# A two-block transformer layer on one core: scan in two stages, choice of tokens in halves, and two hand-overs moved

## The reference, cut to what matters

```python
# mlstm_scan, for a chunk, from the carried state c0, n0, m0
logw = where(tril, cum[:, None] - cum[None, :] + ic[None, :], -inf)
s = (qc @ kc.T) * exp(logw - m)
num = s @ vc + dec * (qc @ c0);  den = s.sum(-1) + dec * (qc @ n0)
hc = num / maximum(abs(den), exp(-m))
c_new = dn * c0 + (wa * kc).T @ vc;  n_new = dn * n0 + (wa * kc).sum(0)
# branch_merge
x = x + ga1 * ((gates[:D] * y_f + gates[D:] * y_m) @ w_out)
# expert_choice, cap = 128 tokens of 1024 for each of 16 experts
aff = softmax(h @ w_router);  vals, idx = top_k(aff.T, cap)
# second block
x = x + mixed @ w_out;  z = rms_norm(x, ln_g) @ w_in      # the next layer
```

## Time and profile before

| | us |
|---|---|
| median of 3 runs (lowest, highest) | 3307.52 (3302.03, 3307.57) |
| profiled execution (its span) | 3307.75 (3305.9) |
| PE busy | 2930.8 (89%) |
| DVE busy | 1666.1 (50%) |
| ACT busy | 1278.3 (39%) |
| POOL busy | 114.2 (3%) |

### The profile page before, as it was taken

How to read it: one execution, slowest core, us unless ns; L and a number is a source line. 1 busy time by engine, 2 the same in 40 slices (tenths; PEclk the granted TensorE clock), 3 DMA queues, 4 the chain that set the end, 5 groups by cost and what they waited for, 6 DMA issues and landing times.

```text
span 3305.9 us, 37686 instructions
## 1 busy us (share of the span) xinstructions
PE 2930.8 (89%) x13860; PEld 2081.0 (63%) x13860; DVE 1666.1 (50%) x3240; ACT 1278.3 (39%) x2362; POOL 114.2 (3%) x154
## 2 busy tenths in 40 slices
PE   7999977899989179999996798799999978999999
PEld 3454456578868156776663575477667865776677
DVE  2127535334335866666662556743652446645523
ACT  2101222223314154554552545643652446535522
POOL 0000000000000001110010000000000000000000
PEclk9999978999989589999998899899999988999999
DMA  9420000022232469999997110020012020200121
GB/s 356 132 77 0 26 26 1 0 102 102 79 139 109 152 222 356 361 363 368 365 363 201 67 26 26 20 59 23 30 52 102 13 77 14 77 1 33 52 77 51
DMA packets 176664, 388.56 MB, mean 118 GB/s; under 512 B 7028, under 2 KB 8084, under 8 KB 176256
## 3 DMA queue, kind: packets, MB, share of 16 engines
q1 hardware_dynamic: 157920, 318.79, 27.6%
q0 software_dynamic: 18448, 67.72, 6.2%
q10 hardware_dynamic: 144, 0.01, 0.0%
HBM read 354.98 MB, written 31.51 MB: 117 GB/s over the span
## 4 chain that ended last, share of the span: by engine, by line
PE 80%; DVE 8%; ACT 5%; DMA 4%; issue 2%; SPq 1%; POOL 0%; DVEq 0%; POOLq 0%; ACTq 0%
PE psum L292 19%; PE psum L699 7%; PE psum L701 7%; PE psum L700 7%; PE psum L1215 4%; PE psum L1331 4%; PE psum L1217 4%; PE psum L1216 4%; PE psum L1349 3%; PE psum L1160 3%; PE psum L1159 3%; PE psum L1158 3%; PE psum L1378 2%; PE psum L1426 2%; PE psum L1428 2%
## 5 line engine op out<-in xcount | busy, mean ns | idle before, releaser
L700 PE MATMUL psum<-ring_r,kctx_r 128*128 128x512 f32 (+1 forms) x544 | 214.7, 395 | 0.0
L700 PE MATMUL psum<-ring_r,cols_r 128*128 128x512 f32 (+1 forms) x544 | 212.5, 391 | 0.0
L1746 ACT ACTIVATE ring<-ring,att 128x256 f32<-128x256 f32 (+7 forms) x256 | 173.1, 677 | 65.7 <-DVE att L2288 65.6
L1331 PE MATMUL psum<-wide 64*128 64x512 f32 (+2 forms) x704 | 158.6, 535 | 21.2 <-DVE att L2288 18.2
L292 PE MATMUL psum<-hidden,ring 128*128 128x512 f32 x384 | 167.4, 597 | 5.8 <-DVE wide L2045 3.8
L2157 DVE TENSOR_TENSOR ring_r<-ring,pair_r 128x1024 fp32r<-128x1024 f32 x128 | 148.0, 1218 | 23.8 <-ACT pair_r L1647 23.8
L1216 PE MATMUL psum<-ring_r,wide_r 128*128 128x512 f32 x384 | 151.3, 394 | 0.0
L1349 PE MATMUL psum<-ident,ring 128*128 128x128 f32 x640 | 122.3, 299 | 26.6 <-ACT sel_wT L1758 16.1
L1349 PEld LDWEIGHTS psum<-ident,ring 128*128 128x128 f32 x640 | 69.8, 145 | 106.8 <-issue 70.7
L292 PEld LDWEIGHTS psum<-hidden,ring 128*128 128x128 f32 x384 | 73.4, 192 | 96.7 <-issue 94.5
L699 PE MATMUL psum<-small_r,kctx_r 128*128 128x512 f32 (+1 forms) x240 | 101.1, 421 | 29.4 <-DVE ring_r L682 20.4
(11 more groups left out here) (447 smaller groups left out, 6842.4 us busy)
## 6 DMA issues: line engine op xcount, KB each, us to landing
ring<-in_w_gate SPq DMA_DIRECT2D x64, 1024.0 KB, 8.9
ring<-in_w_up SPq DMA_DIRECT2D x32, 1024.0 KB, 9.4
hidden<-in_w_up SPq DMA_DIRECT2D x32, 1024.0 KB, 9.1
hidden<-in_w_down SPq DMA_DIRECT2D x32, 1024.0 KB, 7.2
pair<-in_w_down SPq DMA_DIRECT2D x32, 1024.0 KB, 7.9
ring<-in_w_ada SPq DMA_DIRECT2D x24, 1024.0 KB, 12.0
ring<-in_w_in SPq DMA_DIRECT2D x24, 1024.0 KB, 7.3
ring<-in_even_w_in SPq DMA_DIRECT2D x16, 1024.0 KB, 15.7
```

The costliest lines, as they stand in the source:

```text
L700: self.eng.matmul(outp, XHIGH[b][:, k, :], low[:, k, 0:wd], start=False, stop=False)
L1331: mm = pe.matmul(bank(2 * (q % 2) + h)[:, 0:n], qT2[row, c, span(b)], kT2[row, 0 if name == "C" else c, k:k + n], start=True, stop=not dia ...
L1746: act.activation(sv, sv, ACT.Exp, bias=nmx[:, q:q + 1], scale=-1.0, accum_out=esum[:, r:r + 1]).then_inc(S(name + "_e"), 1)
```

## The change

Five things change. (1) In the scan, PE, ACT and DVE run one step's first part (`scan_first`, `scan_weigh`, `scan_scores`) ahead of the step before's second part (`scan_second`, `scan_carried`, `scan_ends`); the banks are dealt out anew, ACT scales the state's product into one of two buffers, and DVE adds three heads in one instruction. (2) The first row block of the output projection is split within the last merge pass, ahead of the weight pieces; PE no longer waits for the sums; POOL loads gain and rows when the last gate group is done. (3) The scores lie as 32 rows of 512 tokens, 16 experts times two halves. Each half's 128 largest are found in descending order; the second half's list is reversed, and the larger of each pair is taken. (4) The residual is stored by row blocks, in both layers. (5) The last two norms between the attention layers, `last_norms_*`, run beside the first two products of the next projection, whose rows and weights are now split by `next_job` within the output projection.

PE in the scan, one round of seven rows, before: the values' product and the increment of one step, then scores, decay rows, transposes and the state's product of the next.

The diff, cut to its core. Of the scan on PE and DVE only the new code is shown, since the old stands above:

```diff
-ob = small[:, 5384:5384 + NH * VW].rearrange("p (h n) -> p h n", h=NH)
+obs = [small[:, o:o + NH * VW].rearrange("p (h n) -> p h n", h=NH) for o in (5384, 5984)]
...
-affT = ctx_hidden[0:NEXP, 0:SEQ]
+affT = ctx_hidden[0:2 * NEXP, 0:HALF]
...
+def heads3(b, last):
+    return [bank(b)[:, h * VW:(h + 1) * VW] for h in range(3)] + [last]
+scan_i = heads3(3, bank(5)[:, 0:VW])
+scan_u = heads3(4, bank(5)[:, VW:2 * VW])
+scan_d = heads3(6, bank(7)[:, 0:VW])
...
     pool.wait_ge(S("ada_out"), 16)
-    pool.wait_ge(S("mg_add"), 16)
+    pool.wait_ge(S("mg_br"), 32)
+    pool.dma_start(ga1b, scratch["ada"][2 * D:3 * D].partition_broadcast(P)).then_inc(S("ga1"), 16)
     for i in range(4):
         pool.dma_start(x1[:, 2 * i:2 * i + 2, :], a["x"].rearrange("(t p) n -> p t n", p=P)[:, 2 * i:2 * i + 2, :]).then_inc(S(f"x_again{i}"), 16)
-    pool.dma_start(ga1b, scratch["ada"][2 * D:3 * D].partition_broadcast(P)).then_inc(S("ga1"), 16)
+    pool.wait_ge(S("mg_add"), 16)
     pool.dma_start(ga2b, scratch["ada"][5 * D:6 * D].partition_broadcast(P)).then_inc(S("ga2"), 16)
...
     for layer in range(2):
-        if layer == 0:
-            pool.wait_ge(S("xb"), TT)
-        else:
-            pool.wait_ge(S("wo0_ev"), before("wo0_ev") + 2 * TT)
         rows = scratch[("xb", "x3")[layer]].rearrange("(t p) n -> p t n", p=P)
-        pool.dma_start(rows, (x1, x3)[layer]).then_inc(S(f"res{layer}_out"), 16)
+        for t in range(TT):
+            if layer == 0:
+                pool.wait_ge(S("xb"), t + 1)
+            else:
+                pool.wait_ge(S("wo0_ev"), before("wo0_ev") + TT + t + 1)
+            pool.dma_start(rows[:, t, :], (x1, x3)[layer][:, t, :]).then_inc(S(f"res{layer}_out"), 16)
...
     pe.wait_ge(S("c_zero"), 2)
...
+    def scan_first(i):
+        d, c, has = steps[i]
+        no = outs_before[i]
+        if i >= 1:
+            pe.wait_ge(S("scan_kw"), 4 * i)
+        for h in range(NH):
+            mm = pe.transpose(bank(2)[:, span(h)], ksrc(h, c), ident[:])
+        mm.then_inc(S("scan_kt"), 1)
+        if not has:
+            return
+        if no >= 1:
+            pe.wait_ge(S("scan_e"), 4 * no)
+        pe.matmul(bank(1), identb[:], maskb[:, d * NH * P:(d + 1) * NH * P], start=True, stop=False, skip_group_check=True)
+        for h in range(NH):
+            mm = pe.matmul(bank(1)[:, span(h)], sel[:, (4 * d + h) * P:(4 * d + h + 1) * P], rR[:, span(c)],
+                           start=False, stop=(h == NH - 1), skip_group_check=True)
+        mm.then_inc(S("scan_r"), 1)
+        if no >= 1:
+            pe.wait_ge(S("scan_se"), no)
+        for h in range(NH):
+            mm = pe.matmul(bank(0)[:, span(h)], ksrc(h, c), qT[:, h, span(c - CT)], start=True, stop=True)
+        mm.then_inc(S("scan_s"), 1)
+    def scan_second(i):
+        d, c, has = steps[i]
         no = outs_before[i]
         if has:
...
+            pe.wait_ge(S("scan_c"), 4 * (i - 1))
             if no >= 1:
...
+                pe.wait_ge(S("scan_o"), no)
             for h in range(NH):
...
+                pe.matmul(scan_i[h], qT[:, h, span(c - CT)], Cst[:, 4 * d + h, :], start=True, stop=True)
+            pe.wait_ge(S("scan_se"), no + 1)
             for h in range(NH):
...
+                mm = pe.matmul(scan_u[h], se[:, no % 2, h, :], vex[:, c, h, :], start=True, stop=True)
+            mm.then_inc(S("scan_u"), 1)
+        pe.wait_ge(S("scan_kw"), 4 * (i + 1))
         if i >= 1:
             pe.wait_ge(S("scan_c"), 4 * i)
         for h in range(NH):
...
+            mm = pe.matmul(scan_d[h], kw[:, i % 2, h, :], vex[:, c, h, :], start=True, stop=True)
         mm.then_inc(S("scan_d"), 1)
+    for i in range(len(steps) + 1):
+        if i < len(steps):
+            scan_first(i)
+        if i >= 1:
+            scan_second(i - 1)
...
     pe.wait_ge(S("mg_sig"), 32)
-    pe.wait_ge(S("mg_mul"), 32)
-    pe.wait_ge(S("mg_add"), 16)
...
-    for t in range(TT):
-        mm = pe.transpose(bank(1 + t // 4)[0:NEXP, (t % 4) * P:(t % 4 + 1) * P], aff[:, t, :], ident[:])
+    for t in range(TT // 2):
+        mm = pe.transpose(bank(1)[0:2 * NEXP, span(t)], aff[:, 2 * t:2 * t + 2, :].rearrange("p t e -> p (t e)"), ident[:])
     mm.then_inc(S("affT"), 1)
     pe.wait_ge(S("topk"), 1)
-    pe.transpose(bank(3)[:, 0:NEXP], vals, ident[0:NEXP, 0:NEXP])
-    pe.transpose(bank(3)[:, NEXP:2 * NEXP], idxf, ident[0:NEXP, 0:NEXP]).then_inc(S("picked"), 1)
+    for i, v in enumerate((vals, idxf, valr, idxr)):
+        mm = pe.transpose(bank(3)[:, 2 * NEXP * i:2 * NEXP * (i + 1)], v, ident[0:2 * NEXP, 0:2 * NEXP])
+    mm.then_inc(S("picked"), 1)
...
-        if layer == 0:
-            N4.transposes(pe, TT - 2)
-            N4.transposes(pe, TT - 1)
...
-    N4.done(pe, TT - 1)
-    qk_pe("cq", "ck")
+    def last_norms_pe(i):
+        if i < 2:
+            N4.transposes(pe, TT - 2 + i)
+            N4.done(pe, TT - 2 + i)
+    qk_pe("cq", "ck", late=last_norms_pe)
...
+    def scan_carried(i):
+        d, c, has = steps[i]
+        no = outs_before[i]
+        if not has:
+            return
+        act.wait_ge(S("scan_u"), no + 1)
+        if no >= 2:
+            act.wait_ge(S("scan_out"), no - 1)
+        for h in range(NH):
+            g = chain_row(d, h)
+            ins = act.activation(obs[no % 2][:, h, :], scan_i[h], ACT.Copy, scale=colv[:, c, 2, g:g + 1])
+        ins.then_inc(S("scan_ob"), 1)
...
+        if t + 1 == len(PASSES):
+            act.wait_ge(S("mg_add"), 14)
+            s2.rows(mT[:, :, span(0)])
...
+    def last_norms_act(i):
+        if i < 2:
+            N4.evac_act(act, TT - 2 + i)
+        if i == 1:
+            act.wait_ge(S("res1_out"), before("res1_out") + 16 * TT)
+        if i == 2:
             N4.done(act, TT - 1)
...
+    def scan_scores(i):
+        d, c, has = steps[i]
         no = outs_before[i]
+        if not has:
+            return
+        dve.wait_ge(S("scan_s"), no + 1)
+        dve.wait_ge(S("scan_e"), 4 * (no + 1))
+        if no >= 2:
+            dve.wait_ge(S("scan_u"), no - 1)
+        dve.scalar_tensor_tensor(se[:, no % 2, :, :], bank(0).rearrange("p (h n) -> p h n", h=NH), KSC,
+                                 ee[:, no % 2, :, :], ALU.mult, ALU.mult).then_inc(S("scan_se"), 1)
+    def scan_ends(i):
+        d, c, has = steps[i]
+        no = outs_before[i]
+        ob = obs[no % 2]
         if has:
...
+            dve.wait_ge(S("scan_ob"), no + 1)
+            dve.tensor_tensor(ob[:, 0:3, :], ob[:, 0:3, :], bank(4)[:, 0:3 * VW].rearrange("p (h n) -> p h n", h=3), ALU.add)
+            dve.tensor_tensor(ob[:, 3, :], ob[:, 3, :], scan_u[3], ALU.add).then_inc(S("scan_o"), 1)
         dve.wait_ge(S("scan_d"), i + 1)
+        if i >= 2:
+            dve.wait_ge(S("scan_c"), 4 * (i - 1))
         for h in range(NH):
...
+            dve.scalar_tensor_tensor(Cst[:, 4 * d + h, :], Cst[:, 4 * d + h, :], dnb[:, 4 * d + h, c:c + 1], scan_d[h],
                                      ALU.mult, ALU.add).then_inc(S("scan_c"), 1)
...
+        if not has:
+            return
+        dve.wait_ge(S("scan_o"), no + 1)
+        g0 = chain_row(d, 0)
+        link(dve.scalar_tensor_tensor(rec, ob[:, :, DH], -1.0, colv[:, c, 3, g0:g0 + NH], ALU.mult, ALU.max))
+        link(dve.tensor_tensor(rec, rec, ob[:, :, DH], ALU.max))
+        link(dve.reciprocal(rec, rec))
+        if no:
+            dve.wait_ge(S("scan_out"), no)
+        hv = hsum[:, c - CT, :].rearrange("p (h n) -> p h n", h=NH)
...
+        ins.then_inc(S("scan_out"), 1)
+    for i in range(len(steps) + 1):
+        if i < len(steps):
+            scan_scores(i)
+        if i >= 1:
+            scan_ends(i - 1)
...
         if key == "fm":
             for c in range(3):
                 merged(c)
+        if t + 1 == len(PASSES):
+            s2.rows(mT[:, :, span(0)])
         for p in range(4):
             if t + 1 < len(PASSES):
                 m2.weights(t + 1, p)
...
-    s2.rows(mT[:, :, span(0)])
...
-    link(dve.tensor_copy(affT, psum[0:NEXP, HALF:3 * HALF]))
+    link(dve.tensor_copy(affT, bank(1)[0:2 * NEXP, :]))
     for r in range(CAP // 8):
         v = vals[:, 8 * r:8 * r + 8]
         link(dve.max(v, affT))
         link(dve.max_index(idx[:, 8 * r:8 * r + 8], v, affT))
-        link(dve.match_replace(affT, v, affT, -1.0))
-    dve.tensor_copy(idxf, idx).then_inc(S("topk"), 1)
+        if r < CAP // 8 - 1:
+            link(dve.match_replace(affT, v, affT, -1.0))
+    link(dve.tensor_copy(idxf, idx))
+    link(dve.tensor_copy(valr, vals[:, ::-1]))
+    dve.tensor_copy(idxr, idxf[:, ::-1]).then_inc(S("topk"), 1)
     dve.wait_ge(S("picked"), 1)
-    link(dve.tensor_copy(valc, bank(3)[:, 0:NEXP]))
-    dve.tensor_copy(idxc, bank(3)[:, NEXP:2 * NEXP]).then_inc(S("route"), 1)
+    link(dve.tensor_copy(both, bank(3)[:, 0:P].rearrange("p (a h e) -> p a h e", a=4, h=2)))
+    v0, i0, v1, i1 = both[:, 0, 0, :], both[:, 1, 0, :], both[:, 2, 1, :], both[:, 3, 1, :]
+    link(dve.tensor_tensor(firsts, v0, v1, ALU.is_ge))
```

(22 more changed lines are left out.)

137 lines of the change are left out of this document (51 added, 86 removed).

## The result

The changed kernel takes 3167.51 us (median of 4 runs, 3165.58 to 3172.30) against 3307.55 us of the kernel before (4 runs on the same chip, 3302.03 to 3312.31): a ratio of 0.9579, 95% interval 0.9560 to 0.9598. The profiled execution of the changed kernel was the slowest of its four (3172.30 us, span 3170.5), so the two traces differ by 135.45 us only, and the other 4.6 us of the 140.0 lie in the spread of the runs.

What follows compares the result with a forecast made beforehand. TensorE and DMA were taken as full in the experts' loop, so time returns only where TensorE waits or runs slow. 65 + 17 + 25.7 + 13.7 = 121.4 us off 3307.75 gave 3186 us, range 3168 to 3222.

Steps and rivals of the forecast that it cites:

- What bounds: Whole kernel: TensorE and DMA are full in the experts' loop; time returns only where TensorE waits or is slow-clocked, four stretches.
- The scan: Scan: TensorE's own work becomes the longest, 5.7 us a step, 115 us against 180.2: -65 us, bounds -73 and -40.
- ring of waits: Scan: engines waiting on each other in a circle; the check claimed none closes, with 1.2 to 2.2 us to spare.
- issue and waits: Scan: 0.3 us a step added to TensorE's 5.40 us of work, making 5.7.
- The slack: Scan: TensorE's inputs ready early, the addition by 1.2 us, the state by 2.0, the scores by 2.2.
- rival B: Scan stays at half clock: TensorE 10.8 us a step, 82 us more, 3268 us; chance 0.07.
- Merge to projection: Merge to first output projection: earlier loads and split, TensorE's two waits gone; -17 us, bounds -19 and -12.
- Choice of tokens: Choice of tokens: passes over 512 columns instead of 1024, 0.53 us saved a pass; -25.7 us, bounds +0.3 and -29.5.
- rival C: Choice of tokens doesn't shorten, its three operations costing by the instruction: 26 us more, 3212 us; chance 0.06.
- Between the layers: Between the attention layers: row-wise stores, earlier splits, later norms; TensorE idles 3.8 us; -13.7 us, bounds -17 and -8.
- Costed at nothing: The first residual's row-wise store, hidden by the first attention layer's projections, and the shared semaphores: no gain or loss.
- Rivals A and D: Scan: A, bound by VectorE and hand-overs, 7.5 us a step, 3215, chance 0.15; D, ring closes, 18.7 us, 3394, 0.03.

Runs made afterwards that it cites:

- dve_scales: The changed kernel, but VectorE instead of ScalarE scales the state's product in the scan: 3169.71 us, ratio 0.9586.
- one_stage: The changed kernel, but in the scan each engine does both stages of a step before the next step: 3182.05 us, ratio 0.9627.
- early_transposes: The kernel before, with each scan step's four key transposes first and the sums laid out as in the changed kernel: 3257.43 us, ratio 0.9852.
- loads_as_before: The changed kernel, but GpSimd loads only when all 16 sums are there, the gain row behind the 4 MB of x: 3186.11 us, ratio 0.9637.
- fewer_waits: The changed kernel with three waits eased: for evacuations and norms between the layers, and the merge's last sum ahead of the fourth weight piece: 3162.70 us, ratio 0.9566.
- late_stores: The changed kernel, but the second layer's eight residual stores are issued only after the last evacuation: 3170.20 us, ratio 0.9592.

## Why the prediction was right, point by point

**What bounds.** Right: time came back where PE stood or ran at 1.2 GHz, and in all four places. The total is less well met than the terms: 140.0 us are more than the 138 of all good ends together, and the time fell 0.5 us below the range. The far end, 3222, is given without its sum; the bad ends named in the four terms (40, 12, none and 8) make 60 us, 3248.

**The scan.** Right in what bounds the new scan, PE's own work with no ring of waits; wrong in size: -75.5 us lies beyond my better bound of -73. Of the missing 10.5 us, 4.7 are the steps (15 from first to last scores took 80.81 us, I had 85.5: 5.51 against 5.7, and the first of them 3.7, since no products of a step before stand in it); 3.0 are the half clock that I charged to output steps and that didn't come (PEclk 1.00 from 452.19 on); 2.6 are the context steps, whose last increment now runs behind the first scores, and in which the clock rose while I had them at half throughout; 0.2 the drain. Two increments show the rise, 1.93 us and 1.13:

```profile
443.65 1.93 PE L1157 MATMUL psum<-wide,small 128*128 128x129 f32 x8
...
446.95 1.13 PE L1157 MATMUL psum<-wide,small 128*128 128x129 f32 x8 [0.52 <-ACT small L1605]
```

The 0.3 us a step for "issue and waits" was 0.1. The slack that I worked out was real: dve_scales put 1.1 us a step more on VectorE at no cost. What I did not see is where the gain sat. I priced the new order as a whole, as the work of two stages side by side; that is worth 13.7 us by one_stage, while early_transposes shows that 46.1 us hung on transposes that stood behind the state only for a shared bank. That the term came near was no proof of its reason.

**On the clock.** 1.00 in the output steps against 0.85, so rival B fell. Before, with 3.5 us of standing in a step of 9.28 and no pause over 2.27 us in the output steps, the clock went to and fro, 0.85 on average; with some 1.1 us in 6.97 it averaged 0.97 and fell twice; with 0.45 in 6.22, and later 0.7 in 6.48, it stayed at 1.00, and with next to none in 5.51 too. The page "TensorE: Matmul & The Clock Gate" of the Trainium skill, section "HAM oscillation — how this bites in real kernels", has a loop whose matmuls wait for their input fall back to 1.2 GHz in every round. The trace of before agrees in that the clock fell again and again, though not in every step.

**Merge to projection.** 17.9 against 17; PE stood 1.36 us between products 0 and 1 where I had 1.9, and product 2 came 12.8 us after the merge where I had 13.1. But my text treated the split of block 0 and the dropped waits as gains of their own; loads_as_before shows that without the early gain row they are worth nothing, and that putting it back behind the rows of x, a place in GpSimd's queue that I did not price, costs 12.3 us, two thirds of what the term gave.

**Choice of tokens.** 26.3 against 25.7. The pass of 0.68 us was right to the nanoseconds shown (682), also for FIND_INDEX8 and MATCH_REPLACE8, so rival C fell.

**Between the layers.** 13.5 against 13.7, with the steps as forecast: 3.34 us of idle time for 3.8, and two waits for norms of 1.3 us for 1.2. That most of this standing was not needed for product 2 I had not seen; fewer_waits took out 6.2 us. The early row-wise stores that I took to belong to the gain did nothing (late_stores).

**Costed at nothing.** The first residual's stores and the shared semaphores had no run of their own, and no difference above points to them. Other stretches with unchanged instructions did move, up to 5.4 us and both ways; for that the forecast had no term. Rivals A and D fell with 5.51 us a step.

**The sum.** 121.4 + 10.5 (scan) + 0.9 (merge) + 0.6 (choice) - 0.2 (layers) = 133.2 by the rows, 2.2 in unchanged stretches, 4.6 between the profiled executions and the medians: 140.0.

## What to carry to other kernels

Before pricing a new order of a whole loop, look for the one instruction that stands behind a wait only because its buffer is shared, and follow who is idle for it: here four transposes held ScalarE, and through it the exponentials, the scores and PE, and moving them alone gave 46 of 75 us. A request's place in a DMA-issuing engine's queue can matter more than when it is issued: 0.5 MB of gain row, wanted first, stood behind 4 MB, at 12.3 us against 6.2 for asking late. And a wait that is eased can pay little when the next one in line is not eased with it (1.3 us alone, 6.2 with the others), so follow the chain two products further before counting it.
